# Gated linear attention by tiles of two chunks, and a full-height score mask, in a two-layer streaming encoder step on one core

## The reference

```python
b = cumsum(log_a, axis=1)                 # within the chunk
qf, kf = q * exp(b), k * exp(-b)
inter = qf @ S
att = where(tril, qf @ kf.T, 0.0)
out = inter + att @ v
S_new = S * exp(b_last)[..., None] + (k * exp(b_last - b)).T @ v
```

## Time and profile before

| | |
|---|---|
| three executions | 3188.14, 3195.36, 3196.07 us, median 3195.36 us |
| the profiled execution | 3194.04 us, its span 3192.1 us |
| PE busy / weight loads / DVE / ACT / POOL | 95% / 82% / 40% / 27% / 24% of the span |
| mean granted clock of TensorE | 0.960 of full |
| the scan | from 370 us to 455 us |
| the sample part | from 455 us to 501 us |
| the prompt's differential attention | from 1774 us to 2119 us |

### The profile page before, as it was taken

The page is one execution under the profiler, slowest core; times in us unless marked ns, Lnnn a source line. Parts: engine busy times, 40 slices in busy tenths (PEclk is TensorE's granted clock), DMA queues, the critical chain, the costliest instruction groups (busy, mean ns, idle before and its releaser), DMA issues. The chain is left out here.

```text
span 3192.1 us, 41287 instructions
## 1 busy us (share of the span) xinstructions
PE 3029.2 (95%) x15916; PEld 2620.4 (82%) x15916; DVE 1283.2 (40%) x2421; ACT 851.7 (27%) x1712; POOL 759.0 (24%) x847
## 2 busy tenths in 40 slices
PE   8999898989999999999999888988989999999997
PEld 6978567889889998897888677766878999889996
DVE  2156745532222222256313577664262222222227
ACT  2152231232112221122010455544132221112221
POOL 1112110422121122124121343333141221212114
PEclk9999888989999999999999698899999999999998
DMA  4101305111111111101322333257301111111101
GB/s 133 40 27 53 125 8 198 47 47 47 40 46 39 39 46 40 46 27 50 107 95 92 87 93 78 59 190 279 106 27 53 42 46 45 39 39 46 46 27 60
DMA packets 234010, 219.74 MB, mean 69 GB/s; under 512 B 78209, under 2 KB 178434, under 8 KB 233874
## 3 DMA queue, kind: packets, MB, share of 16 engines
q1 hardware_dynamic: 233874, 217.91, 21.6%
HBM read 184.83 MB, written 33.03 MB: 68 GB/s over the span
## 5 line engine op out<-in xcount | busy, mean ns | idle before, releaser
L1243 PE MATMUL ps<-xt,wsplit 128*128 128x384 f32 x5184 | 912.9, 337 | 2.4 <-DVE xt L1678 2.4
L1243 PEld LDWEIGHTS ps<-xt,wsplit 128*128 128x128 f32 x5184 | 909.4, 190 | 5.3 <-issue 2.0
L709 POOL TENSOR_TENSOR wsplit<-raw,wsplit 128x1024 fp32r<-128x1024 f32 x192 | 461.4, 2404 | 1839.2 <-ACT wsplit L880 1839.2
L1414 PE MATMUL ps<-wsplit,hT 128*128 128x512 f32 x3456 | 787.9, 390 | 0.0
L1414 PEld LDWEIGHTS ps<-wsplit,hT 128*128 128x128 f32 x3456 | 649.2, 188 | 134.4
L1261 PE MATMUL ps<-wsplit,xt 128*128 128x512 f32 x3024 | 703.2, 393 | 2.8 <-DVE xt L1678 2.8
L1261 PEld LDWEIGHTS ps<-wsplit,xt 128*128 128x128 f32 x3024 | 571.1, 190 | 128.3 <-issue 6.5
L880 ACT ACTIVATE wsplit<-raw 128x1024 fp32r<-128x1024 f32 x192 | 202.4, 1054 | 970.3 <-PE ps L1414 612.9
L1884 DVE TENSOR_TENSOR x_res<-x_res,ps 128x512 f32<-128x512 f32 x252 | 172.2, 686 | 439.5 <-PE ps L1414 439.5
L1917 DVE TENSOR_SCALAR hsq<-ps 128x384 f32<-128x384 f32 x192 | 106.9, 557 | 562.2 <-PE ps L1243 562.2
L1023 ACT ACTIVATE hsq<-hsq 128x384 f32<-128x384 f32 x192 | 101.1, 527 | 570.9 <-DVE hsq L1917 570.9
(11 more groups left out here) (169 smaller groups left out, 2352.2 us busy)
## 6 DMA issues: line engine op xcount, KB each, us to landing
raw<-in_w_up SPq DMA_DIRECT2D x64, 512.0 KB, 4.0
raw<-in_w_down SPq DMA_DIRECT2D x64, 512.0 KB, 3.6
Kc<-in_cache_k SPq DMA_DIRECT2D x8, 2048.0 KB, 10.6
Vc<-in_cache_v SPq DMA_DIRECT2D x8, 2048.0 KB, 10.1
raw<-in_w_in_a SPq DMA_DIRECT2D x24, 512.0 KB, 3.7
out<-kvs SPq DMA_DIRECT2D x36, 256.0 KB, 2.0
raw<-in_w_kv SPq DMA_DIRECT2D x16, 512.0 KB, 4.3
kqd<-out SPq DMA_DIRECT2D x128, 64.0 KB, 2.1
```

The lines of the kernel that those rows point to most:

```text
L709: nc.gpsimd.tensor_tensor(wsplit[:, slot, 1, :], raw[:, slot, :], wsplit[:, slot, 0, :].bitcast(F32), ALU.subtract).then_inc(lo_done, 1)
L1243: last = nc.tensor.matmul(ps[0:M, b, 0:GW], st, xt[:, c, k, ng * GW:(ng + 1) * GW], start=(k == 0 and i == 0), stop=(k == KT - 1 and i == 2))
L1414: last = nc.tensor.matmul(ps[:, (v + t) % 6, :], hT[:, a, 2 * kp + k, tok:tok + P], wsplit[:, q, b, k * 512:(k + 1) * 512], start=(kp == 0 ...
```

## The change

It does three things.

1. The mask of the prompt's scores: `mrow` becomes 128 rows (the row as before, then 127 rows of zeros) and fp32r, so that the product is a 128-row one in a single pass. It is loaded as float32 (128 KB) into `mask32` and rounded by one ACT instruction near the program's start.
2. The scan goes by tiles. The state is updated once for each tile (by `etile`, the product of the two chunks' last decays, made by one new DVE instruction before the scan). The keys of a whole tile meet the values in one product, with the first chunk's keys decayed by `etile`. The scores now hold the pairs across the two chunks too: the 64 queries of the second chunk meet `kmix`, where the first chunk's keys are multiplied by that chunk's last decay `e0`. The whole tile's queries meet the state before the tile in one product, with the second chunk's multiplied by `e0` (`qdec`). `kmix` and `qdec` are made by POOL, four instructions of 128 by 64 for each step (two in tile 0).
3. The sample part: POOL spreads each head's queries over a block matrix `qblk` (zeros but for each stream's 16 columns, 8 copies of 128 by 16 for each head), and the output comes from products of 128 queries with a stream's state, eight for each head, added onto the masked scores times the values. The transposed products, ACT's copies and the products with the identity go.

The core of the diff (line numbers left out):

```diff
-    m = np.zeros((1, 2 * P), np.float32)
+    m = np.zeros((P, 2 * P), np.float32)
-    mrow = at("mrow", O_C + 2976, [1, 2 * P])
+    mrow = at("mrow", O_C + 2976, [P, 2 * P], F32R)
-    c[:, C_MP:C_MP + P] = (j // CH == i // CH) & (j <= i)
+    c[:, C_MP:C_MP + P] = j <= i
...
# POOL
+        def scan_operands(s):
+            t, h = s // H_A, s % H_A
+            q, k = (qkT[:, i, h, t * P:(t + 1) * P] for i in range(2))
+            e0 = elast[:, h, 2 * t:2 * t + 1]
+            if s >= 2:
+                pool.wait_ge(scan_scores, s - 1)
+            nc.gpsimd.tensor_scalar(kmix[:, s % 2, 0:CH], k[:, 0:CH], e0, None, ALU.mult)
+            nc.gpsimd.tensor_copy(kmix[:, s % 2, CH:P], k[:, CH:P]).then_inc(keys_mixed, 1)
+            if t:
+                if s >= 2:
+                    pool.wait_ge(scan_out, s - 1)
+                nc.gpsimd.tensor_copy(qdec[:, s % 2, 0:CH], q[:, 0:CH])
+                nc.gpsimd.tensor_scalar(qdec[:, s % 2, CH:P], q[:, CH:P], e0, None,
+                                        ALU.mult).then_inc(queries_decayed, 1)
+        nc.gpsimd.memset(qblk[:], 0.0).then_inc(qblk_zero, 1)
+        scan_operands(0)
+        scan_operands(1)
+        for s in range(PT * H_A):
+            if s + 2 < PT * H_A:
+                scan_operands(s + 2)
+            if s >= 2 and s % 2 == 0:
+                power(s // 2 - 1)
+        for h in range(H_A):
+            if h:
+                pool.wait_ge(scan_out, PT * H_A + h)
...
+            for b in range(STREAMS):
+                last = nc.gpsimd.tensor_copy(diagonal[:, b, b * SEQ_S:(b + 1) * SEQ_S], ...)
+            last.then_inc(smp_qblk, 1)
...
# ACT
+        act.wait_ge(tile_decays, 1)
-            for c in range(2):
+            for c, decay in enumerate((etile[:, h, t:t + 1], elast[:, h, 2 * t + 1:2 * t + 2])):
...
# PE, scores
-            nc.tensor.matmul(ps[:, 1, 0:P], qkT[:, 1, h, t * P:(t + 1) * P], qkT[:, 0, h, t * P:(t + 1) * P],
+            nc.tensor.matmul(ps[:, 1, 0:CH], qkT[:, 1, h, t * P:(t + 1) * P], q[:, 0:CH], start=True, stop=True)
+            pe.wait_ge(keys_mixed, s + 1)
+            nc.tensor.matmul(ps[:, 1, CH:P], kmix[:, s % 2, :], q[:, CH:P],
                              start=True, stop=True).then_inc(scan_scores, 1)
# PE, outputs
-            for c in range(2):
-                if s:
-                    pe.wait_ge(state_updated, 2 * (s - 1) + c + 1)
-                nc.tensor.matmul(ps[:, 2 + c, 0:DV], kts[c * CH:(c + 1) * CH, s % 2, :],
-                                 vO[c * CH:(c + 1) * CH, t, h * DV:(h + 1) * DV],
-                                 start=True, stop=True).then_inc(scan_kv, 1)
+            if s >= 2:
+                pe.wait_ge(state_updated, s - 1)
+            nc.tensor.matmul(ps[:, 2 + s % 2, 0:DV], kts[:, s % 2, :], v, start=True, stop=True).then_inc(scan_kv, 1)
...
-                nc.tensor.matmul(o[0:CH], q[:, 0:CH], S[:, 0, h, :], start=False, stop=True, ...)
-            pe.wait_ge(state_updated, 2 * s + 1)
-            nc.tensor.matmul(o[CH:P], q[:, CH:P], S[:, 1, h, :], start=False, stop=True, ...)
+                pe.wait_ge(state_updated, s - 3)
+                pe.wait_ge(queries_decayed, s - 3)
+                last = nc.tensor.matmul(o, qdec[:, s % 2, :], S[:, (t - 1) % 2, h, :], start=False, stop=True)
# PE, sample part
+        pe.wait_ge(smp_masked, 1)
...
+            nc.tensor.matmul(o, attS[:, h, :], vO[:, PT, h * DV:(h + 1) * DV], start=True, stop=False)
+            pe.wait_ge(smp_qblk, h + 1)
             for b in range(STREAMS):
+                last = nc.tensor.matmul(o, qblk[:, b * P:(b + 1) * P], Ss[:, b, h, :],
+                                        start=False, stop=(b == STREAMS - 1))
# DVE: one update for each step (s), with etile; before the scan:
+        nc.vector.tensor_tensor(etile[:], elast[:, :, 0:2 * PT:2], elast[:, :, 1:2 * PT:2], ALU.mult).then_inc(tile_decays, 1)
+        dve.wait_ge(tile_decays, 1)
```

More of the change, by code:

```diff
@@ L211, in encoder_step @@
     attS = at("attS", O_XT + 15360, [P, H_A, P])
-    oT = at("oT", O_XT + 17408, [P, 8, P])
-    ktb = at("ktb", O_XT + 21504, [P, STREAMS, H_A * P])
-    Ss = at("Ss", O_XT + 37888, [P, STREAMS, H_A, DV])
+    ktb = at("ktb", O_XT + 17408, [P, STREAMS, H_A * P])
+    Ss = at("Ss", O_XT + 33792, [P, STREAMS, H_A, DV])
+    kmix = at("kmix", O_XT + 66560, [P, 2, P])
+    qdec = at("qdec", O_XT + 67584, [P, 2, P])
+    etile = at("etile", O_XT + 68608, [P, H_A, PT])
+    qblk = at("qblk", O_XT + 69632, [P, STREAMS * P])
     K_BANK = (4, 5, 7)
@@ L491, in _ @@
         sp.dma_start(gna_g[:], g_norm_a[0:1, :].broadcast_to([P, DV])).then_inc(gna_in, 16)
[L492 removed]
+        sp.dma_start(mask32[:], maskrow).then_inc(mask_in, 16)
         for m in range(4, 8):
@@ L724, in _ @@
             split_lo(g)
-        for p in range(2 * PT + 2):
+        def scan_operands(s):
[12 more added lines that the diff above has]
+                                        ALU.mult).then_inc(queries_decayed, 1)
+        pool.wait_ge(qk_scaled, 3 * H_A * NG)
+        pool.wait_ge(g_full, GU_O)
+        nc.gpsimd.memset(qblk[:], 0.0).then_inc(qblk_zero, 1)
[6 more added lines that the diff above has]
+                power(s // 2 - 1)
+        pool.wait_ge(qblk_zero, 1)
+        for h in range(H_A):
+            if h:
+                pool.wait_ge(scan_out, PT * H_A + h)
+            diagonal = qblk[:].rearrange("p (b n) -> p b n", b=STREAMS)
+            for b in range(STREAMS):
+                last = nc.gpsimd.tensor_copy(diagonal[:, b, b * SEQ_S:(b + 1) * SEQ_S],
+                                             qkT[:, 0, h, PT * P + b * SEQ_S:PT * P + (b + 1) * SEQ_S])
+            last.then_inc(smp_qblk, 1)
+            if h == 0:
+                power(2 * PT - 1)
+        for p in range(2 * PT, 2 * PT + 2):
             power(p)
@@ L900, in _ @@
         nc.scalar.mul(nbg, bg, -1.0).then_inc(nbias_done, 1)
+        act.wait_ge(mask_in, 16)
+        nc.scalar.activation(mrow[:], mask32[:], ACT.Copy).then_inc(mask_rounded, 1)
         for g in range(4, 12):
@@ L988, in _ @@
         last.then_inc(smp_blocks, 1)
[L989 to L993, removed]
         for p in (2 * PT, 2 * PT + 1):
@@ L1845, in _ @@
             mean_square(p)
-        dve.wait_ge(smp_state_out, 1)
+        dve.wait_ge(scan_out, steps + H_A)
         for b in range(STREAMS):
```

72 lines of the change are left out of this document (28 added, 44 removed).

## The result

| | before | changed |
|---|---|---|
| executions of the first comparison, median | 3191.75 us (3183.83 to 3196.07) | 3110.21 us (3105.91 to 3111.47) |
| profiled execution | 3194.04 us | 3110.46 us |
| mean granted clock | 0.960 | 0.974 |

The spans of the two profiled executions, 3192.1 and 3108.5 us, differ by 83.6 us. By places (first scores of the attention, last step's start, as PE's timelines have them), 26.8 us are gained up to the sample part's state products, 1.2 lost on the way to the attention, 55.9 gained in the attention, and 2.1 behind it. No run has the scan's or the sample part's change alone, so their shares are read from these starts, one profiled execution of each kernel. Lines are now those of the changed kernel.

What follows compares the result with a forecast made beforehand. PE's in-order list, busy 95% of the span, was taken as the bound. Scan -18, start +1, sample part -8 and attention masks -28 summed to -53 us from 3194; forecast 3142 us, range 3120 to 3174.

Steps and rivals of the forecast that it cites:

- Scan step: Scan: a step on PE falls from 2.58 to 2.0 us over 32 steps, -18 us (ends -22 and -7).
- Rival A: Scan: GpSimd (POOL) becomes the bound, its pair of instructions taking 0.90 us; scan -7 for -18, 3153 us; 10%.
- Start: Ahead of the scan: the first transpose comes later, waiting for `etile` and ACT, +1 us (0.5 to 2).
- Sample part: Sample outputs: fewer products, but waits for masked scores and three `qblk` refills; -8 us (ends -11 and 0).
- Mask at full clock: Attention: each mask gives PE 0.40 us, partly hidden by waits; 3.0 us a head, 19 us at full clock.
- The clock: Attention: less PE work may bring half clock more often; one more stretch charged, 5.8 us.
- the good end of 40: Attention: -40 us, with no more half clock and half of the lost first masks coming back.
- rival D: Attention: PE waits more in blocks 0 and 1, the clock falls more often, 5.8 us each; 3206 us; 5%.
- Rival B: Scan: the half-array form was better, a step becomes 2.80 us; scan +7, 3167 us; 6%.
- its rule: Scan: the skill's advice to give products with 64 or fewer rows or columns separate array parts, running at once.

Runs made afterwards that it cites:

- b1: Changed kernel with POOL refilling each `qblk` block once its product has read it, and the masked scores' product last in each head; 3103.03 us.
- d1: Changed kernel with one spare DVE product of 128x256 ahead of each `combine` in the attention; 3131.46 us.
- m2: Changed kernel with the old mask product (one row, float32, two passes); 3158.93 us.
- w1: b1 with 13, 4 and 4 spare float32 matmuls of 512 columns in PE's idle times ahead of the attention; 3105.11 us.
- m1: Kernel before with the mask's part of the change alone (128 rows, fp32r, one pass); 3139.14 us.
- m4: Changed kernel with one row of mask in fp32r, so one pass; 3125.85 us.
- m3: Changed kernel with 128 rows of mask in float32, so two passes; 3118.85 us.
- m5: Changed kernel with a mask of 64 rows in float32, two passes; 3142.58 us.
- m6: Changed kernel with the one-row fp32r mask product issued twice; 3148.53 us.
- s1: Changed kernel with the scan's product of queries and state split into two products of 64 output rows each; 3118.78 us.
- w3: b1 with spare float32 matmuls of 512 columns in PE's idle times, 18 ahead of the scan and 7, 2, 2 ahead of the attention; 3101.85 us.

## Why the prediction was wrong, by its steps

- **Scan step**: right. 1.93 us for 2.0. From the transpose to the first product with the values it is 0.50 us (394.97 to 395.47) for the 0.57 of five passes at 0.113: a 64-column pass follows in less than that, 0.17 us for two. `qdec` or `kmix` take 0.64 to 0.66 us on POOL from first start to last end (0.45 for the scaling of 128x64, 0.24 for the copy, overlapping a little) for 0.55, and `power` 0.72 for 0.69; the wait for `kmix` is 0.1 us in every second step, not more. Scan and start together gave 19.9 us for 17, by the start of the sample part's first product (434.87 for 454.72). Rival A's mechanism is there, but too small to count.
- **Start**: 371.49 for 370.35, +1.1 us for +1.
- **Sample part**: 7 us for 8. The waits were as reckoned (2.3 us for the masked scores, 3 x 1.0 for `qblk` with the hand-over); the wait for the scores brought 3 us of half clock (the first head's products took 5.03 us for b1's 3.62), which was in the bounds and not in the sum.
- **Mask at full clock**: the mechanism right, the size low. 0.45 us a mask for 0.40 on PE, since the pass is followed after 0.06 us and not 0.11; 3.7 us a head (38.76 to 35.07) for 3.0. DVE's wait for masks fell from 6.1 to 2.2 us a head, PE's for DVE rose from 3.9 to 5.6. Over the stage, without any half clock, that is 28.2 us (the table); 3.0 a head would be 23.
- **The clock**: this step failed. "Less work on PE may bring the half clock more often; I charge one more, 5.8" had the wrong sign: what is lost to half clock fell from 32.8 to 5.1 us. Those 27.7 us are the other half of the stage's 55.9. My sum for the stage was 19 + 14 - 5.8 = 27.2 (written as 28): in the table's split that is 23 at full clock and 4 by the clock. So of the 28.7 us by which it falls short, 5 are the size of the mask and 23.5 the clock, and even the good end of 40 assumed no shorter time at half clock than before. In the changed kernel the falls still begin in block 0 of a head, where rival D had them, but the clock comes back after 3.4 us and not after 10 to 14. I took PE waiting for DVE as the cause; d1 shows that more of it costs about 1 us of clock, and m2 that the old mask brings most of the loss back (22.4 us). Up to 10 of the 27.7 us may be no effect of the mask, since before and m2 differ by that much. 4 of them are head 0's, where what was lost fell from 7.6 to 3.3 us; its stretch at half clock isn't there in w1, where spare products fill PE's idle time ahead of the stage.

Taken together: the old mask took some 0.5 us of PE's list, 128 times, of which 0.22 streamed. At full clock that is a plain cost; besides, it goes with stretches of half clock that last much longer. The second is shown as a fact (m1, m2); by what property of the mask it comes about is open. Neither gaps alone (m4) nor the second pass alone (m3) nor longer waits (d1) do it; few rows in two passes do, to less extent in m5 and m6 (falls of up to 6.8 us) than with the old mask. What makes the clock fall in block 0 in some heads and not in others, with the same wait, was not tried.

**Rival B and its rule.** s1 measured it: half-array products overlap in pairs and still lost 0.25 us a step. "TensorE: Matmul & The Clock Gate" in the Trainium skill, Part 3, counts the overlap and not what lies around it; in this chain of full-array products the measurement decides against it. The Trainium skill's "TensorEngine Tiling (Array Packing)", section Key Properties, says that changing the tiling mode drains TensorE; the rows agree with it, and have 0.10 us ahead of such a group (s1, m4), and behind it 0.15 (s1) and 0.19 (m4). The Trainium skill's "TensorE: Matmul & The Clock Gate", section "Why this matters for your kernels", says that a single product with 32 rows takes the time of one with 128. No run has 32 rows; with full-height products around it, one row in one pass took 0.58 us where 128 rows took 0.29, from the start of the product ahead of it to the start of the one behind it.

## What to carry to other kernels

In a loop like this one, pad a small product between full-array ones with zeros to full height and make it a single pass: here its neighbours' starts came from 0.74 to 0.29 us apart. Judge a mask, a bias row or a one-row broadcast on PE by the distance between its neighbours' starts, not by its own record. When a stage has time at half clock, split its cost first ("full" and "lost" above): here the edit gave back as much in clock (27.7 us) as in time at full clock (28.2), and a term for the clock in a prediction needs a bound on the good side too.

## What the runs showed of the hardware that I had not expected

- With the old mask the clock needed 10 to 14 us to come back in all seven heads where it fell in block 0 (the traces of before and m2), with 128 rows or one pass 3.4 us, and in m5 and m6 up to 6.8; heads 2.7 us longer by DVE (d1) didn't change it.
- Two costs that are small alone do more than add: 16 us (one row), 9 us (second pass), 49 us (both, of which some 17 are clock).
- A mask of 64 rows in two passes has the gaps of one row within 0.01 us: 0.32 us ahead and 0.42 behind, for 0.33 and 0.41.
- The half clock behind an idle stretch can be avoided with spare products (w1: first head 2.5 us shorter), but in w3 6.8 us at half clock began 1.5 us behind a wait of 1.6 us, and no gain clear of noise was left.
